# Token-major products in 256-column halves, with a 64-column matmul ahead of each unseeded group

## What is computed

```python
h = rmsnorm(x, g_pre_mix[l]) * (1 + scale_m) + shift_m
z = h @ w_in[l]
(q_lat, kv_lat, k_rope, gq, gk, gv, g_lr, g_og, gate_a, gate_b) = jnp.split(z, IN_OFFSETS, axis=-1)
y_a = mla_branch(...) @ w_branch_a[l]
y_b = gla_branch(...) @ w_branch_b[l]
merged = jax.nn.sigmoid(gate_a) * y_a + jax.nn.sigmoid(gate_b) * y_b
y = merged @ w_mix_out[l]
x = x + gate_m * rmsnorm(y, g_post_mix[l])
h = rmsnorm(x, g_pre_ffn[l]) * (1 + scale_f) + shift_f
f = conv_ffn(h, w_ffn_up[l], conv_w[l], conv_b[l], w_ffn_down[l])   # 2048 -> 2 x 5632 -> 2048
x = x + gate_f * rmsnorm(f, g_post_ffn[l])
```

## Time and profile before

| what | value |
| --- | --- |
| median of 3 runs | 1633.57 us (1633.0 to 1634.55) |
| the profiled execution | 1634.93 us, span 1633.1 us |
| TensorE matmuls | 11711, busy 1587.2 us |
| VectorE, ScalarE busy | 1136.0 us, 817.7 us |
| mean granted TensorE clock | 0.992 |

### The profile page before, as it was taken

One profiled execution on the slowest core, in us unless ns is written; L12 is line 12 of the kernel. 1 busy time (PEld: TensorE's weight loads), 2 busy tenths in 40 slices (PEclk: granted clock), 3 DMA queues, 4 the chain that ended last, 5 costly groups with the idle time before them and its releaser, 6 DMA issues.

```text
span 1633.1 us, 29398 instructions
## 1 busy us (share of the span) xinstructions
PE 1587.2 (97%) x11711; PEld 1492.6 (91%) x11711; DVE 1136.0 (70%) x1323; ACT 817.7 (50%) x1064; POOL 7.3 (0%) x11
## 2 busy tenths in 40 slices
PE   3999999999999999999998999999999999999998
PEld 2999999879999999999887999999999999888886
DVE  6778767887877696877756577777777665544444
ACT  4557766656444643434445454545454544443332
POOL 0000000000000000000000000000000000000000
PEclk9899999999999999999999999999999999999999
DMA  8999978875459897877864577777777656555554
GB/s 297 321 326 335 321 265 241 303 249 181 123 161 300 273 296 246 285 272 267 319 239 130 182 238 244 242 243 236 235 243 234 196 188 212 187 185 197 189 190 144
DMA packets 197150, 389.33 MB, mean 238 GB/s; under 512 B 18487, under 2 KB 31545, under 8 KB 196297
## 3 DMA queue, kind: packets, MB, share of 16 engines
q1 hardware_dynamic: 192457, 371.38, 68.3%
q10 hardware_dynamic: 4610, 16.79, 3.0%
HBM read 386.02 MB, written 2.10 MB: 238 GB/s over the span
## 4 chain that ended last, share of the span: by engine, by line
PE 93%; DVE 3%; DMA 2%; ACT 1%; issue 1%; SPq 0%; DVEq 0%; ACTq 0%
PE ps L558 20%; PE ps L562 20%; PE ps L560 20%; PE ps L585 8%; PE ps L587 8%; PE ps L586 8%; PE ps L743 2%; DMA ada<-in_w_ada 2%; DVE w_lo L1314 1%; DVE acc L1337 1%; PE ps L682 1%; ACT w_hi L913 0%; PE ps L533 0%; PE ps L634 0%; PE ps L650 0%
## 5 line engine op out<-in xcount | busy, mean ns | idle before, releaser
L1314 DVE TENSOR_TENSOR w_lo<-raw,w_hi 128x1024 fp32r<-128x1024 f32 x530 | 625.5, 1221 | 442.1 <-ACT w_hi L913 441.4
L913 ACT ACTIVATE w_hi<-raw 128x1024 fp32r<-128x1024 f32 x530 | 532.8, 1052 | 674.1 <-PE ps L562 442.8
L558 PE MATMUL ps<-h2t,w_hi 128*128 128x256 f32 x1408 | 391.1, 278 | 0.0
L562 PE MATMUL ps<-h2t,w_lo 128*128 128x256 f32 x1408 | 390.0, 277 | 0.0
L560 PE MATMUL ps<-h2t,w_hi 128*128 128x256 f32 x1408 | 389.9, 277 | 0.0
L558 PE MATMUL ps<-ht,w_hi 128*128 128x256 f32 x1136 | 319.9, 282 | 0.0
L562 PE MATMUL ps<-ht,w_lo 128*128 128x256 f32 x1136 | 316.4, 279 | 0.0
L560 PE MATMUL ps<-ht,w_hi 128*128 128x256 f32 x1136 | 316.4, 279 | 0.0
L560 PEld LDWEIGHTS ps<-h2t,w_hi 128*128 128x128 f32 x1408 | 265.6, 189 | 0.0
L558 PEld LDWEIGHTS ps<-h2t,w_hi 128*128 128x128 f32 x1408 | 265.0, 188 | 0.0
L562 PEld LDWEIGHTS ps<-h2t,w_lo 128*128 128x128 f32 x1408 | 264.9, 188 | 0.0
(11 more groups left out here) (271 smaller groups left out, 1997.9 us busy)
## 6 DMA issues: line engine op xcount, KB each, us to landing
raw<-in_w_ffn_up SPq DMA_DIRECT2D x176, 512.0 KB, 4.5
raw<-in_w_in SPq DMA_DIRECT2D x168, 512.0 KB, 5.1
ada<-in_w_ada SPq DMA_DIRECT2D x160, 512.0 KB, 6.6
raw<-in_w_ffn_down SPq DMA_DIRECT2D x88, 512.0 KB, 4.2
raw<-in_w_branch_b SPq DMA_DIRECT2D x32, 512.0 KB, 5.2
raw<-in_w_mix_out SPq DMA_DIRECT2D x32, 512.0 KB, 5.3
ada<-in_w_ada ACTq DMA_DIRECT2D x32, 512.0 KB, 4.1
raw<-in_w_branch_a SPq DMA_DIRECT2D x16, 512.0 KB, 5.5
```

The costliest lines, as they stand in the source:

```text
L558: mm(o, w_hi[:, s, k, cols], moving[:, kt, 0], start=opens, stop=False, skip_group_check=True)
L562: ins = mm(o, w_lo[:, s, k, cols], moving[:, kt, 0], start=False, stop=stop, skip_group_check=True)
L913: A(w_hi[:, slot], raw[:, slot], ACT.Copy).then_inc(hi_done, 1)
L1314: V.tensor_tensor(w_lo[:, slot], raw[:, slot], w_hi[:, slot].bitcast(F32), ALU.subtract)\
```

## The change

In `token_pair` each product is taken in two halves of 256 columns: the outer loop goes over the halves, then over slots and contraction tiles as before, and each matmul takes half of the weight block's columns into half of the bank. Only the very first matmul of an unseeded group has `start=True`. Ahead of an unseeded group's first tile stands a call of `pace`. Nothing else is touched.

```diff
                 for t in range(NT):
                     if first:
                         tile_free(t0 + t, None if seed is None else seed + t)
-                    o = ps[:, bank0 + t, :]
-                    for j in range(2):
-                        s = (slot + j) % RING
-                        for k in range(2):
-                            kt = kt0 + 2 * j + k
-                            tok = slice(t * P, (t + 1) * P)
-                            opens = first and seed is None and j == 0 and k == 0
-                            mm(o, still[:, kt, 0, tok], w_hi[:, s, k, :], start=opens, stop=False, skip_group_check=True)
-                            mm(o, still[:, kt, 0, tok], w_lo[:, s, k, :], start=False, stop=False, skip_group_check=True)
-                            ins = mm(o, still[:, kt, 1, tok], w_hi[:, s, k, :], start=False,
-                                     stop=last and j == 1 and k == 1, skip_group_check=True)
+                    tok = slice(t * P, (t + 1) * P)
+                    if first and seed is None and t == 0:
+                        pace(still, bank0)
+                    for half in range(2):
+                        cols = slice(half * S, (half + 1) * S)
+                        o = ps[:, bank0 + t, cols]
+                        for j in range(2):
+                            s = (slot + j) % RING
+                            for k in range(2):
+                                kt = kt0 + 2 * j + k
+                                opens = first and seed is None and half == 0 and j == 0 and k == 0
+                                mm(o, still[:, kt, 0, tok], w_hi[:, s, k, cols], start=opens, stop=False,
+                                   skip_group_check=True)
+                                mm(o, still[:, kt, 0, tok], w_lo[:, s, k, cols], start=False, stop=False,
+                                   skip_group_check=True)
+                                ins = mm(o, still[:, kt, 1, tok], w_hi[:, s, k, cols], start=False,
+                                         stop=last and j == 1 and k == 1, skip_group_check=True)
                     if last:
                         ins.then_inc(tile_ready, 1)
```

## The result

The changed kernel took 1651.14 us (median of 4 runs, 1648.77 to 1653.01), the kernel before 1634.06 us beside it: a ratio of 1.0102 with a 95% interval of 1.0086 to 1.0118. The forecast was 1630.8 us in a range up to 1641. The profiled execution of the change has a span of 1650.2 us, 17.1 us more than before.

A forecast was written before the change was run, and what follows sets the result against it. TensorE, busy 97% of the span, was taken as the bound. Last stage -1.8, mix -0.4, gv -0.4 and +0.3, og -0.4 sum to -2.7 us: 1633.57 becomes 1630.8 us, range 1628.8 to 1641.

The forecast's parts named there:

- the three speeds: TensorE streams: 228.9 ns per 512-column token-major product; 113.4 fast or 117.8 slow per 256-column feature-major product.
- The counts: In last stage, mix and gv, 1824 matmuls become 3648 of 256 columns, plus 12 openers of 64 columns.
- the FFN's distance (113.4 ns): Feature-major FFN's fast stretch: 113.4 ns per 256-column product; lengths of feature-major stages from 897 to 1380 must stay.
- Rival 1: Halves open slow and stay slow: +7.6 us in the last stage alone, 1640.3 us, or 1648 if all; chance 0.20.
- Does the opener put the stream into the fast speed?: Last stage: opener behind gate_rows was taken to give fast halves; stage 239.9 us with openers, 1.8 us less.
- The mix and gv terms: Token-major mix and gv passes: fast halves plus openers save 0.4 us each; 0.3 added for seeded gv pairs.
- A slow first mix group: If mix's first group opened slow, 192 matmuls at 4.5 ns each would lose 0.9 us.
- the eight seeded gv pairs: Of twelve seeded pairs without opener, eight stand behind attention's small fp32 matmuls; 0.3 us added for twelve, bounds 0 and 2.6.
- a first distance of 0.31 us: Behind attention's wider fp32 matmuls, 522.87 to 523.18: said to give weight loads a lead, so gv pairs run fast.
- The og term: Og passes at 104.5 to 114.5 us, behind gv: fast instead of 118.2 ns, saving 0.4 us; bounds 0 and 0.4.
- The rule against it: Trainium skill's N / 2.4 + 2.5 ns per warm matmul: the split would cost 4.6 us over 1824 matmuls.
- the weight load, just covered by 256 columns: A 128-column load takes 107 ns, just covered by a 256-column product; said to show as two speeds there.

The follow-up runs named there:

- fast-entry kernel: The change without openers in token_pair, last-stage loop written out, gate_rows moved ahead of the last FFN group; 1635.34 us, ratio 1.0012 to the kernel before.
- 1649.8 us: The change without its 64-column openers: 1649.8 us, ratio 1.0104 to the kernel before; the theory that moving weight blocks are slow by nature forecast 1649.5.

## Why the prediction was wrong

- **Right:** the three speeds, and that the split would be decided by which of the two it ran at. The measured 117.8 and 113.4 are those of the earlier trace rows. The counts and the FFN's distance (113.4 ns) were right too. Rival 1, halves that open slow and stay slow, priced at 1648 us for all stages, is what happened; it had 0.20. That its total comes within 3 us of 1651 is in part luck: it lacks 5.6 us in the last stage (below), and mix and what lies ahead came out cheaper than it had them.
- **The step that failed:** "Does the opener put the stream into the fast speed?", with its end "So I take 'down' as fast". It took the opener's effect from feature-major groups to token-major ones, where no row showed it. There it does the opposite. Each fast stream that met an opener ahead of token-major halves was slow behind it, eight of eight (64, 128 and 256 columns of the own form, 64 of the weight-tile form), and no opener tried made a slow token-major stream fast. For the last stage the step failed twice over: gate_rows alone left it slow at 117.8 ns, where the prediction had read from the groups behind the earlier gate_rows (113.5 ns) that it would open fast. Which of the two made the changed kernel's last stage slow can't be told, as either is enough; in mix it was the opener.
- **The mix and gv terms** (-0.4 each) failed by the same step. Without openers mix is entered fast, as the sum had it, though the late split can end that: slow in two of the three profiled executions of the fast-entry kernel. A slow first mix group was priced at 0.9 us, as if the next opener would mend it; none did, and all 768 halves cost 3.4. Of the eight seeded gv pairs between attention's matmuls, which I took as fast from the earlier trace rows, six were slow in the change's trace. The sign read from those rows, a first distance of 0.31 us, wasn't there: in halves it was 0.20 to 0.23, behind a 256-column fp32 matmul too (315.28).
- **The og term** (-0.4) was right for the products it names: behind halves those at 104 us opened fast. But the same reasoning left out the 384 products at 184 us, which lost 1.7 us.
- **A term that was missing:** the jump back. I checked which instructions the loop holds and not how many. The doubled body cost 3.1 us of gap and about 2.5 of half clock, nearly all of the 5.8 us by which the last stage exceeds rival 1's price of 7.6. Written out, the stage took 5.8 us less.
- **A sum:** with every term at its worst bound (openers 0.2 us, gv 2.6, og nothing) the prediction's own terms reach 1634.4 us, not 1632.8. It doesn't matter beside the step that failed.
- **The rule against it** (a fixed price per matmul) isn't the cause: without openers and with a fast entry two halves cost 226.8 ns against 228.9. That the weight load, just covered by 256 columns, makes the two speeds was argued; no run tested it.
- **What stays open:** why an opener slows down token-major streams, and why feature-major ones behave otherwise. There only the traces speak, no run without those openers: a slow feature-major stream was fast behind each of 17 openers inside it. The spread of the fast-entry kernel's twelve times (up to 1640.75) was explained only in part, by mix and by the clock ahead of the branches.

## What to carry to other kernels

Where a stream of equal matmuls has two speeds in a trace, a trick that sets the fast one is measured on the operand form in which it stands; its effect on another form is unknown until a trace shows it. The slow speed costs 4.5 ns per half, 9 per product, and the split can win only 2.1 ns per product (228.9 less 226.8), so a few slow stretches decide its sign. The stretches behind the changed code can change speed as well, so they are read too. Where executions differ by more than the change, a total can even match the wrong theory, as 1649.8 us did; the distance in the stretch tells them apart. And when a loop body is doubled, count its instructions and look for fetches in the second iteration: the profile can put a gap at the jump down to a wait that did not cause it.

## What the runs showed of the hardware

- A stream of 256-column fp32r products with a weight load each runs at 113.3 or 117.8 ns at the full clock, and kept the one it was entered with, over as many as 2112 products. Idling, a late operand or another matmul in between can change it. Much of this repeats: the two seeded gv passes that start at 170 to 174 us, behind small matmuls of other work, were slow in all nine traces with halves in gv. Some of it doesn't: mix of the same kernel had both speeds in different executions.
- A loop body of 1056 TensorE instructions ran its second iteration without a fetch. One of about 2112 was fetched again, with 2.96, 3.25 and 3.35 us from start to start at the jump in the three traces that have it; behind it the clock stood at its 1.2 GHz level for 3.4 us in two of them, and in the change's trace from within the gap for 6.8 us. Where between the two sizes the limit lies was not tried.
- 512-column products of the last stage stayed at 228.6 to 228.9 ns, behind gate_rows, behind an opener, and behind feature-major products.
